# Second value rows and head gates in one product of 152 columns, unit-matrix turns at the attention's end, and buffers at multiples of 512 bytes

## The reference

```python
proj = h @ w_in
q_a, kv_a, gate_a, qkv_b, merge = jnp.split(proj, IN_SPLITS, axis=-1)
k_cmp, v_cmp, k_sel, v_sel, k_win, v_win = (kv_a[i] for i in range(6))
g_a = sigmoid(gate_a)                      # 3 gates for each of 8 heads: 24 columns
o_a = g_a[..., 0:1] * o_cmp + g_a[..., 1:2] * o_sel + g_a[..., 2:3] * o_win
y_a = o_a @ w_proj_a
o_b = stick_breaking(qkv_b[0], qkv_b[1], qkv_b[2])
y_b = o_b @ w_proj_b
y = sigmoid(merge[:, :, 0]) * y_a + sigmoid(merge[:, :, 1]) * y_b
```

## Time and profile before

| | us |
|---|---|
| median of three runs | 1800.1 (1797.98 to 1800.95) |
| the profiled execution's own time | 1799.04 |
| its span on the core | 1797.3 |
| PE busy | 1691.2 (94%) |
| DVE busy | 805.1 (45%) |
| ACT busy | 544.2 (30%) |

### The profile page before, as it was taken

One profiled execution on the slowest core, in us unless ns is written; L12 is line 12 of the kernel. 1 busy time (PEld: TensorE's weight loads), 2 busy tenths in 40 slices (PEclk: granted clock), 3 DMA queues, 4 the chain that ended last, 5 costly groups with the idle time before them and its releaser, 6 DMA issues. The chain is left out here.

```text
span 1797.3 us, 20148 instructions
## 1 busy us (share of the span) xinstructions
PE 1691.2 (94%) x8185; PEld 1175.5 (65%) x8185; DVE 805.1 (45%) x1245; ACT 544.2 (30%) x899; POOL 49.8 (3%) x89
## 2 busy tenths in 40 slices
PE   4999999889989999999999999998999988888898
PEld 3888756568878888888788876766343433333456
DVE  6673567654632223365622464244332323232345
ACT  5112366633362222232533450423100000000036
POOL 0000011000000000000000000000200000000000
PEclk9999999989999999999999999999999999999999
DMA  9865210011723332211422021247899999999971
GB/s 374 269 256 162 94 71 1 2 55 64 238 71 103 104 94 94 105 71 48 164 94 94 1 94 48 97 168 305 311 427 424 426 426 425 426 426 425 426 299 48
DMA packets 87400, 351.76 MB, mean 196 GB/s; under 512 B 8246, under 2 KB 39650, under 8 KB 70921
## 3 DMA queue, kind: packets, MB, share of 16 engines
q1 hardware_dynamic: 84418, 346.02, 49.5%
q0 software_dynamic: 2560, 4.37, 0.7%
q10 hardware_dynamic: 328, 0.06, 0.0%
HBM read 346.03 MB, written 8.43 MB: 197 GB/s over the span
## 5 line engine op out<-in xcount | busy, mean ns | idle before, releaser
L594 DVE TENSOR_TENSOR arena<-ring,arena 128x1024 fp32r<-128x1024 f32 x120 | 146.8, 1225 | 229.6 <-ACT arena L651 206.5
L2989 PE MATMUL ex_h<-ring,u_big_tail 128*64 128x512 f32 x544 | 162.1, 610 | 12.6 <-DMA ring<-in_w 6.7
L599 PE MATMUL up_ps<-h_high,arena 128*128 128x512 f32 x352 | 138.1, 392 | 2.9 <-DVE arena L594 2.9
L601 PE MATMUL up_ps<-h_high,arena 128*128 128x512 f32 x352 | 137.5, 391 | 0.0
L600 PE MATMUL up_ps<-arena 128*128 128x512 f32 x352 | 137.4, 390 | 0.0
L651 ACT CAST arena<-ring 128x1024 fp32r<-128x1024 f32 x81 | 84.8, 1047 | 149.5 <-PE up_ps L601 82.2
L2989 PE MATMUL ex_h<-s_ab,u_big_tail 128*64 128x512 f32 x304 | 121.4, 596 | 1.5 <-DVE u_big_tail L2960 1.5
L2989 PEld LDWEIGHTS ex_h<-ring,u_big_tail 128*64 128x64 f32 x544 | 49.7, 139 | 83.2 <-issue 82.1
L2960 DVE TENSOR_TENSOR u_big_tail<-ex_x,vcol 128x512 f32<-128x512 f32 x32 | 20.6, 686 | 177.9 <-PE ex_x L2953 177.9
L3312 ACT ACTIVATE u_big_tail<-ex_h 128x512 f32<-128x512 f32 x16 | 9.6, 598 | 281.2 <-PE ex_h L2989 281.2
L599 PEld LDWEIGHTS up_ps<-h_high,arena 128*128 128x128 f32 x352 | 66.4, 189 | 18.6 <-DVE arena L594 3.3
(11 more groups left out here) (609 smaller groups left out, 3658.5 us busy)
## 6 DMA issues: line engine op xcount, KB each, us to landing
ring<-in_w SPq DMA_DIRECT2D x40, 2048.0 KB, 31.7
s_ab<-in_w SPq DMA_DIRECT2D x32, 2048.0 KB, 32.0
ring<-in_w_in SPq DMA_DIRECT2D x18, 2048.0 KB, 8.5
ring<-in_w_ada SPq DMA_DIRECT2D x24, 1024.0 KB, 7.0
reg_a<-in_w SPq DMA_DIRECT2D x10, 2048.0 KB, 31.9
w1flat<-in_w SPq DMA_DIRECT2D x10, 2048.0 KB, 33.0
ring<-in_w_ffn_gate SPq DMA_DIRECT2D x11, 1024.0 KB, 5.7
ring<-in_w_ffn_up SPq DMA_DIRECT2D x11, 1024.0 KB, 8.3
```

The source lines that it names most:

```text
L594: return engine.tensor_tensor(lo, v, hi.bitcast(F32), ALU.subtract)
L599: nc.tensor.matmul(ps, x[0], y[0], start=start, stop=False)
L601: return nc.tensor.matmul(ps, x[1], y[0], start=False, stop=stop)
L2989: mm = nc.tensor.matmul(ps[half, :], xT[:, k, half], ws[j][:, k, cols], start=(k == 0), stop=(k == k_end - 1))
```

## The change

- The window values and the gates are 152 neighbouring columns of one chunk. The tiles ("rows", window values) and ("gate") become two tiles "both", each of 2 groups of 128 tokens by 8 products of 152 columns. ACT evicts the first and DVE the second, with two copies each (24 and 128 columns).
- In `turn` the wait for the copy out of `ps_t` now comes before the wait for the weights, and in the steps 43 to 47 four transposes of the unit matrix into `ps_t` stand between them. After the last spread, twelve such transposes go into a score bank. Their results are never read.
- In the merge ACT waits for the last scores (the region in which the side parts lie held the keys until then), makes sides 0 and 1, and only then waits for `y_made`.
- `lead` grows by 8 words and a `trail` of 120 words is put at the top, so that the large buffers on both sides start at multiples of 512 bytes. `tri` moves into the first part of `g1row`, which is no longer in use then.

```diff
--- before.py
+++ after.py
@@ -60,7 +60,8 @@
 NEG = -1e30
 MASKED = -1e33
 SP_CAP = 60.0
-LEAD = 88
+LEAD = 96
+TRAIL = 120
 FIRST = 256
 FIRST_PART = -1
 
@@ -104,6 +105,7 @@
         self.passing = []
         self.block = None
         self.lead = self.sb("lead", [P, LEAD])
+        self.trail = self.ctx.enter_context(nc.sbuf_tensor("trail", [P, TRAIL], F32, side="right"))
         self.ring_at = nc.sbuf_base
         self.ring = self.sb("ring", [P, RING, 8 * CH])
         self.reg_a_at = nc.sbuf_base
@@ -790,14 +792,15 @@
 
     tiles = [(0, n * P, "q", b.qT[:, n, :]) for n in range(4)]
     tiles += [(1, 0, "dup", b.kvc[0]), (1, P, "dup", b.kvc[1]), (1, 2 * P, "dup", b.kk[0]), (1, 3 * P, "rows", b.vv[0])]
-    tiles += [(2, 0, "dup", b.kk[1]), (2, P, "rows", b.vv[1]), (2, 2 * P, "gate", b.gate)]
+    BOTH = P + 24
+    tiles += [(2, 0, "dup", b.kk[1])] + [(2, P, "both", slice(2 * i, 2 * i + 2)) for i in range(2)]
     tiles += [(3, n * P, "q", b.sqT[:, n, :]) for n in range(4)]
     tiles += [(4, n * P, "T", b.skT[:, n, :]) for n in range(4)]
     tiles += [(5, t, "wide", b.sv[:, t, :]) for t in range(4)]
     NB = 6
     def directs(i):
 
-        return sum(t[2] in ("rows", "gate") for t in tiles[:i + 1])
+        return sum(t[2] in ("rows", "both") for t in tiles[:i + 1])
 
     b.acc2 = b.ring[:, 3]
     direct, ev_a, ev_d, cleared, bias_in, added = (b.sem(f"p1_{n}") for n in ("direct", "eva", "evd", "cleared", "bias", "added"))
@@ -865,7 +868,7 @@
 
         @block.tensor
         def _(pe):
-            for i, (c, n0, kind, _) in enumerate(tiles):
+            for i, (c, n0, kind, dst) in enumerate(tiles):
                 if i >= NB and not (kind == "wide" and n0):
                     pe.wait_ge((ev_d, ev_a)[i % 2], (i - NB) // 2 + 1)
                 bank = ps[i % NB]
@@ -878,15 +881,15 @@
                 elif kind != "wide":
                     w = b.chunk(b.c_in[c])
                     b.wait_chunk(pe, b.c_in[c])
-                    n = P if kind == "rows" else 24
-                    for t in range(NT):
-                        mm = product_rows(nc, bank[:, t * n:t * n + n], b.hT, t, w[:, :, n0:n0 + n], KD)
+                    n = P if kind == "rows" else BOTH
+                    for at, t in enumerate(range(NT) if kind == "rows" else range(dst.start, dst.stop)):
+                        mm = product_rows(nc, bank[:, at * n:at * n + n], b.hT, t, w[:, :, n0:n0 + n], KD)
                 elif n0 == 0:
                     for j in range(1, NT):
                         pe.wait_ge((ev_d, ev_a)[(i + j) % 2], (i + j - NB) // 2 + 1)
                     for j in range(4):
                         parts.pe_rows(pe, unit_of[i] + j, [ps[(i + t) % NB] for t in range(NT)], 2 * j)
-                if kind in ("rows", "gate"):
+                if kind in ("rows", "both"):
                     mm.then_inc(direct, 1)
                     if i + 1 < len(tiles) and tiles[i + 1][0] != c:
                         pe.wait_ge(direct, directs(i))
@@ -923,7 +926,9 @@
             elif kind == "rows":
                 last = copy(dst, bank[:].rearrange("p (t n) -> p t n", t=NT))
             else:
-                last = copy(dst[:], bank[:, 0:NT * 24].rearrange("p (t n) -> p t n", t=NT))
+                out = bank[:, 0:2 * BOTH].rearrange("p (t n) -> p t n", t=2)
+                copy(b.gate[:, dst, :], out[:, :, P:BOTH])
+                last = copy(b.vv[1][:, dst, :], out[:, :, 0:P])
             last.then_inc(done, 1)
 
         @block.gpsimd
@@ -1335,7 +1340,7 @@
         ps_t = banks("t", 2)
         ps_o = [banks(f"o{i}", 1) for i in range(2)]
         block = b.block
-        b.at_y = y_made
+        b.at_y, b.at_scored = y_made, (scored, 2 * N)
 
         @block.sync
         def _(sp):
@@ -1359,14 +1364,20 @@
                     ks = b.skT[r, n, 0:k] if kind == 2 else b.kk[kind][r, n // 2, 0:k]
                     nc.tensor.matmul(ps_s[i % 2][:, e, 0:k], q, ks, start=True, stop=True).then_inc(scored, 1)
 
-            def turn(g):
+            def idle_turns(bank, n):
+
+                for _ in range(n):
+                    nc.tensor.transpose(bank, b.ident[:], b.ident[:])
+
+            def turn(g, idle):
                 i = back[g]
+                if g:
+                    wait_copied(pe, g - 1)
+                idle_turns(ps_t[:, 0, 0:P], idle)
                 if stick(i):
                     pe.wait_ge(p_stick, sticks.index(i) + 1)
                 else:
                     pe.wait_ge(p_soft, softs.index(i) + 1)
-                if g:
-                    wait_copied(pe, g - 1)
                 for e in range(2):
                     for c in range(units[i][0] + 1):
                         mm = nc.tensor.transpose(ps_t[:, e, c * P:c * P + P], buf(i)[:, e, c * P:c * P + P], b.ident[:])
@@ -1396,7 +1407,7 @@
                     r = block_end(s, LAG + 4)
                     if r is not None:
                         pe.wait_ge(shared, r + 1)
-                    turn(g)
+                    turn(g, 4 if N - 5 <= s < N else 0)
                 if behind(s, LAG + 1) is not None:
                     values(behind(s, LAG + 1))
                 r = block_end(s, LAG + 3)
@@ -1408,6 +1419,8 @@
                             mm = nc.tensor.matmul(ps_t[:, kind, n * P:n * P + P], wide[kind][:, n * P:n * P + P], b.ident[:],
                                                   start=True, stop=True)
                     mm.then_inc(spread, 1)
+            pe.wait_ge(taken, 2 * len(softs))
+            idle_turns(ps_s[0][:, 0, 0:P], 12)
 
         @block.vector
         def _(dve):
@@ -1650,11 +1663,12 @@
 
         @block.scalar
         def _(act):
+            act.wait_ge(*b.at_scored)
+            act_side(act, 0, 0)
+            act_side(act, 0, 1)
             act.wait_ge(b.at_y, NT)
-            act_side(act, 0, 0)
             for k in range(4):
                 act_y(act, 0, k)
-            act_side(act, 0, 1)
             parts.act_w(act, 0)
             for k in range(KD):
                 act_side(act, 0, k + 2)
@@ -2211,7 +2225,7 @@
 
 def stage_gmlp(b):
 
-    b.tri = b.sb("tri", [P, P])
+    b.tri = b.g1row[:, 0:P]
 
 
 def stage_hgrn(b):
```

## The result

The changed kernel took 1784.8 us (median of 3 runs, 1784.5 to 1786.8) against 1800.1 us: a ratio of 0.9919, with a 95% interval of 0.9896 to 0.9941. That is 15.3 us faster where 6.5 us against that median were forecast (5.4 us between profiled executions), and under the range's low end of 1787.5. The profiled execution has a span of 1783.0 us against 1797.3.

A forecast was written before the change was run, and what follows sets the result against it. The prediction took the tensor engine (PE), busy 94% of the span, and its clock as deciding, with DMA full in the expert stage. Gains of 1.6 + 2.4 + 0.6 + 0.8 = 5.4 us gave 1793.6 us, range 1787.5 to 1799.0.

The forecast's parts named there:

- Products of 152 columns: Projection: 64 records of 128 and 64 of 24 columns become 64 of 152, taking 8.4 us; 1.6 us gained.
- The gap: Projection, third unit behind the wide products: PE idles from 109.9 to 115.35 us for DVE, then restarts at half clock.
- it does not come sooner: Projection: the slab's transfer, landing at 111.61 us, waits for a buffer that DVE frees, so stays as late.
- Turns in the drain: Attention's end: four unit-matrix turns in each of five steps keep PE's clock up; 2.4 us gained if it holds.
- behind the spread: Before the first merge product: twelve turns fill about 1.4 us of PE's 5.01 us idle time; 0.8 us gained.
- Casts ahead: Before the merge: the scalar engine makes two side casts ahead of the attention's last result; 0.6 us gained.
- Alignment costed at nothing: Buffers moved 32 bytes higher, to multiples of 512 bytes: no gain or cost counted.
- Engines do not care: Alignment term: rows with shifted or oddly placed operands take about as long, so buffer addresses cost engines nothing.
- rival B: Expert stage: transfers gain from the alignment, 431 GB/s throughout, 4.7 us more gained, 1788.9 us; chance 0.09.
- A: Attention's drain and merge start: the clock is not held, only 1.0 us gained in all, 1798.0 us; chance 0.26.
- C: Projection keeps all it saves, as the slab's transfer comes sooner: up to 9.0 us from part 1, 1786.2 us; chance 0.05.
- D: Expert stage: transfers at the common 512-byte offset meet PE's reads more often, 410 GB/s, 1809.2 us; chance 0.04.

The follow-up runs named there:

- e5: Kernel before with only the products of 152 columns, plus 60 already-met waits at PE's start: 1795.9 us, ratio 0.9985.
- e3: Kernel before with only the products of 152 columns: 1801.1 us, ratio 1.0008.
- e2: Changed kernel with its buffers back at the old addresses, without the alignment: 1790.0 us, ratio 0.9956 against the kernel before.
- e16_no_turns: Changed kernel without its unit-matrix turns, waits in the old order, 60 already-met waits at PE's start instead: 1788.7 us, ratio 0.9939 against the kernel before.
- e1_align: Kernel before with only the alignment: buffers at multiples of 512 bytes and the triangle in the row buffer: 1795.2 us, ratio 0.9978.
- e7: Kernel before with nothing but 188 already-met waits at PE's start: 1799.6 us.
- e8: Changed kernel with 128 already-met waits at PE's start: 1793.9 us.

## Why the prediction was wrong

1. **Products of 152 columns (1.6): right.** The records take 8.4 us as forecast. The gap is 4.95 us (5.4 forecast), and the clock behind it is 0.51 for 4.5 us (4.3 forecast, with 0.47 of their length lost). Alone they are worth 1.4 us by e5 and some 3.1 by e3, once the stretch over the jump is taken out. By single profiles the projection's end is 0.9 to 1.1 us earlier with the part alone (e3, e5), 2.3 without the alignment (e2) and 2.9 in the whole. One reading failed: "it does not come sooner" of the slab's transfer. It landed at 109.79 and not 111.61 us in the changed kernel and released PE at 113.86; without the alignment the release was at 115.62 (e3) and 116.07 (e5), beside 115.35 forecast.
2. **Turns in the drain (2.4) and behind the spread (0.8): right as a sum.** 3.2 forecast together, 2.2 to 3.8 measured; the two were not run apart. That the clock would hold was argued from the earlier trace rows against the Trainium skill (TensorE: Matmul & The Clock Gate, "Part 4: PE-mode transpose"), by which a transpose does not count as the engine being busy in the same way; e16_no_turns at 0.60 and the changed kernel at 0.95 side with the rows. Behind the spread the clock did fall, at 367.42 us, but for 3.4 us and not the 6.8 before. I priced the turns as if the old drain were always cold; it was in six of nine.
3. **Casts ahead: right as far as can be told,** 0.6 forecast, 0.6 in the medians, inside the noise, and 0.7 by the traces.
4. **Alignment costed at nothing: the first failed step.** It brings 4.1 us alone and 5.2 in the whole. "Engines do not care" may hold, but it was an argument about engines, and I let the mean rate of the earlier trace rows stand as a bound for transfers. That was rival B, at 0.09, with its mechanism right and its 4.7 us in the expert stage a little high: e1_align's profile has that stage 3.8 us shorter than the kernel before, and the first projection product 0.9 us earlier. That its ceiling of 431 GB/s, the best slice, came so near the new mean of 430 was luck: the slices scatter as widely after as before, so the scatter was no sign of the address.
5. **The place of the code: no term at all, the second failed step.** The prediction counted each instruction's time and never where the count moves later code. For this change that was luck twice over: over the jump, the wide products alone run 5.0 us longer than the kernel before and the turns alone 6.2. Both together lose nothing, and even remove the 0.93 us wait of the kernel before, which is worth 2.0 us over the jump (by the whole expert stage 1.7 in e7 and 2.1 in e2 and e5; with the 3.8 of e1 that is the 5.7 us found there). At the place of e8 the change would have looked some 7 to 9 us worse.
6. **The sum:** 4.1 to 5.2 for the alignment, 1.4 to 3.1, 2.2 to 3.8, 0.6, and 2.0 for the removed gap are 10.3 to 14.7 us of 15.3. The rest is within the errors of these numbers (each about 1 us or more) and is not explained further.

Rivals A, C and D: the clock was held in the drain, the gap was there, and the expert stage's transfers ran faster and not slower at the common offset.

## What to carry to other kernels

Where a part's effect has the wrong sign, look at the timeline for a wait "<-issue" behind a jump before believing it: count the instructions that an edit adds ahead of it, and measure edit and base at the same place of the code, with met waits as filler, few enough to fit into a wait (60 instructions did here, 128 did not). Put buffers that take large transfers at multiples of 256 bytes: worth 0.9% of the rate here. And price a clock that falls in some executions and not in others from several of them, not from one.

## What the runs showed of the hardware

- Code comes in transfers of about 16.4 KB (256 instructions of PE). A jump over 206 instructions cost nothing (nine profiles at 188, one at 220), a wait of 0.67 to 0.96 us 18 products on (five at 0) or 5.2 to 5.5 us at the target (three at 60 and 128), by its place in them, with 3.4 or 6.8 us at half clock behind the long ones. All of this was in a stage with full DMA engines; no run has the jump elsewhere.
- Large transfers reach 426 GB/s at 480 and 448 past a multiple of 512 bytes, and 430 at 0 and 256.
- With unit-matrix turns TensorE's granted clock was 0.90 or more in nine of nine drains; without, it was 0.60 to 0.74 in six of nine.
- 128 added instructions of met waits put PE's first product at 15.6 us and 188 at 22.1, where it came at 12.5 without any and at 12.6 with 60.
